# A feed-forward stage's VectorE order rearranged, with the low parts of 12 weight products moved from GpSimd to VectorE

## The reference, cut to what matters

```python
u = relu(rmsnorm(x, ln2) @ w_ff1)      # 1024 -> 4096
x = x + (u * u) @ w_ff2                # 4096 -> 1024
return rmsnorm(x, ln_f)
```

## Time and profile before

| | us |
|---|---|
| runs | 2685.26, 2678.33, 2684.0 |
| median | 2684.0 |
| the profiled execution, its own time | 2677.82 |
| its span, first to last instruction | 2676.0 |
| feed-forward stage in it, product 0 to the last matmul | 2019.6 to 2667.1 |

### The profile page before, as it was taken

How to read it: one execution, slowest core, us unless ns; L and a number is a source line. 1 busy time by engine, 2 the same in 40 slices (tenths; PEclk the granted TensorE clock), 3 DMA queues, 4 the chain that set the end, 5 groups by cost and what they waited for, 6 DMA issues and landing times. The chain is left out here.

```text
span 2676.0 us, 32703 instructions
## 1 busy us (share of the span) xinstructions
PE 2603.0 (97%) x13315; PEld 2193.7 (82%) x13315; DVE 1366.9 (51%) x1550; ACT 1094.1 (41%) x1700; POOL 814.7 (30%) x326
## 2 busy tenths in 40 slices
PE   7899999999999999999999999999998999999998
PEld 6688898898888888888888889888886788787877
DVE  3456633662332223564552667334427865838478
ACT  4356631111222212636563666333424535334344
POOL 1111112221222222422212225321423464555554
PEclk9899999999999999999999999999999999999999
DMA  3000011111111113222112113410125253351611
GB/s 134 24 25 25 25 40 48 47 48 40 44 51 41 50 48 112 73 105 71 40 40 87 53 49 131 165 56 32 40 79 216 99 202 144 126 220 34 249 63 63
DMA packets 68674, 216.77 MB, mean 81 GB/s; under 512 B 5476, under 2 KB 5860, under 8 KB 63672
## 3 DMA queue, kind: packets, MB, share of 16 engines
q1 hardware_dynamic: 63728, 190.53, 20.4%
q10 hardware_dynamic: 4808, 24.29, 2.4%
HBM read 185.23 MB, written 25.38 MB: 79 GB/s over the span
## 5 line engine op out<-in xcount | busy, mean ns | idle before, releaser
L711 POOL TENSOR_TENSOR w_lo<-w_raw,w_hi 128x1024 fp32r<-128x1024 f32 x144 | 349.0, 2424 | 1247.4 <-ACT w_hi L1862 1247.2
L851 POOL TENSOR_TENSOR ff_wl<-ff_raw,ff_wh 128x1024 fp32r<-128x1024 f32 x112 | 336.4, 3026 | 350.1 <-ACT ff_wh L2665 350.1
L864 PE MATMUL ps<-A_hi,w_hi 128*128 128x512 f32 (+2 forms) x1064 | 281.8, 357 | 0.0
L864 PE MATMUL ps<-A_lo,w_hi 128*128 128x512 f32 (+2 forms) x1064 | 279.3, 355 | 0.0
L864 PE MATMUL ps<-A_hi,w_lo 128*128 128x512 f32 (+2 forms) x1064 | 279.1, 354 | 0.0
L1862 ACT ACTIVATE w_hi<-w_raw 128x1024 fp32r<-128x1024 f32 x144 | 151.7, 1054 | 224.7 <-PE ps L864 131.2
L864 PEld LDWEIGHTS ps<-A_hi,w_hi 128*128 128x128 f32 x1064 | 182.7, 189 | 29.3 <-issue 1.9
L864 PEld LDWEIGHTS ps<-A_lo,w_hi 128*128 128x128 f32 x1064 | 182.8, 189 | 28.1
L864 PEld LDWEIGHTS ps<-A_hi,w_lo 128*128 128x128 f32 x1064 | 182.5, 189 | 27.9
L2665 ACT ACTIVATE ff_wh<-ff_raw 128x1024 fp32r<-128x1024 f32 x112 | 112.3, 1050 | 222.3 <-PE ps L1843 211.4
L1843 PE MATMUL ps<-ff_wh,A_hi 128*128 128x512 f32 x448 | 178.3, 398 | 13.6 <-DVE ff_y L3646 10.2
(11 more groups left out here) (530 smaller groups left out, 5920.5 us busy)
## 6 DMA issues: line engine op xcount, KB each, us to landing
w_raw<-in_units SPq DMA_DIRECT2D x144, 512.0 KB, 3.2
ff_raw<-in_blocks SPq DMA_DIRECT2D x32, 1024.0 KB, 4.8
A_hi<-token_operands SPq DMA_DIRECT2D x21, 1024.0 KB, 5.2
A_lo<-token_operands SPq DMA_DIRECT2D x21, 1024.0 KB, 7.2
token_operands<-A_hi SPq DMA_DIRECT2D x7, 1024.0 KB, 6.5
token_operands<-A_lo SPq DMA_DIRECT2D x7, 1024.0 KB, 8.2
X<-in_x ACTq DMA_DIRECT2D x4, 1024.0 KB, 12.1
X<-in_x ACTq DMA_DIRECT2D x1, 4096.0 KB, 15.4
```

Source lines behind the costliest of these rows:

```text
L711: nc.gpsimd.tensor_tensor(w_lo[:, slot, :], w_raw[:, slot, :], w_hi[:, slot, :].bitcast(F32), ALU.subtract).then_inc(w_lo_ready, 1)
L851: nc.gpsimd.tensor_tensor(ff_wl[n % 2][:, 2 * e:2 * e + 2, :], src[:, 2 * e:2 * e + 2, :], ff_wh[n % 2][:, 2 * e:2 * e + 2, :].bitcast(F32 ...
L864: last = nc.tensor.matmul(out, w[:, slot, o:o + m], v[:, k, cols] if k is not None else v[:, cols], start=(first and j == 0 and q == 0), s ...
```

## The change

- DVE makes the weights' low parts of the products n with m odd and j = 0, 1, 2 (12 of 56, in two halves each); `weight_low(n + 1)` stands right behind block 0's addition of product n. POOL skips them and waits, at the product after them, until they are all made.
- In iteration j = 0 of a second matrix the additions of blocks 0 and 1 move up among the sums: s3, block 0, low part, s2, block 1, s4, square_low(g, 2), block 2, block 3.
- Ahead of the stage ff_sum "c" and "e" move between ln2_low(5) and ln2_low(6), and token_low(0) moves between the two steps of `tok_t4`. ACT's token_high(0) moves from the end of iteration 0 into iteration 1, behind ff_high(2) and the last take of product 0. The norm's buffers swap places, so that ff_sum "e" overwrites only the gains and the squares.

```diff
+def ff_low_on_dve(n):
+
+    return n // 7 % 2 == 1 and n % 7 < 3
+
-        ln2_t = norm_temps("ln2", 49152)
+        ln2_t = (ar("ln2_g", 53248, [P, D]), ar("ln2_xn", 57344, [P, 2, D]), ar("ln2_sq", 49152, [P, D]))
...
                 src = ff_raw[FF_RAW[m][FF_ROLE[j]]]
+                if ff_low_on_dve(n):
+                    continue
+                if n and ff_low_on_dve(n - 1):
+                    pool.wait_ge(ff["wl"], fb["wl"] + 2 * n)
...
+                if n == 1:
+                    token_high(0)
                 for b in range(3):
                     ff_take(n, b)
-                if n < 4:
+                if 1 <= n < 4:
                     token_high(n)
...
             ln2.xn()
-            for o in range(4, ST):
-                ln2_low(o)
...
+            def weight_low(n):
+
+                src = ff_raw[FF_RAW[n // 7][FF_ROLE[n % 7]]]
+                for e in range(2):
+                    dve.wait_ge(ff["wh"], fb["wh"] + 2 * n + e + 1)
+                    if e == 0:
+                        dve.wait_ge(ff["wl"], fb["wl"] + 2 * n)
+                    v.tensor_tensor(ff_wl[n % 2][:, 2 * e:2 * e + 2, :], src[:, 2 * e:2 * e + 2, :],
+                                    ff_wh[n % 2][:, 2 * e:2 * e + 2, :].bitcast(F32), ALU.subtract).then_inc(ff["wl"], 1)
...
+            ln2_low(4)
+            ln2_low(5)
             dve.wait_ge(sw["w_xo"], 2 * ST)
-            dve.wait_ge(ff["t2"], fb["t2"] + 4)
             ff_sum(0, "c")
             ff_sum(0, "e")
+            ln2_low(6)
+            ln2_low(7)
+            dve.wait_ge(ff["t2"], fb["t2"] + 4)
             hi_21, lo_21 = (quadrant(a, 1).bitcast(F32) for a in (A_hi, A_lo))
             v.tensor_tensor(tok_t4[:, :, :], hi_21, tok_t2[:, :, :], ALU.subtract).then_inc(ff["t4"], 1)
+            token_low(0)
...
                 if second and j == 0:
-                    for kind in ("s3", "s2", "s4"):
-                        square_sum(g, kind, 1)
+                    square_sum(g, "s3", 1)
...
                 if taken:
                     ff_add(n, 0)
+                if n + 1 < FF_N and ff_low_on_dve(n + 1):
+                    weight_low(n + 1)
                 if first and j == 4:
                     square_low(g, 0)
+                if second and j == 0:
+                    square_sum(g, "s2", 1)
...
                 if second and j == 0:
+                    square_sum(g, "s4", 1)
                     square_low(g, 2)
...
-                if n < 4:
+                if 1 <= n < 4:
                     token_low(n)
```

## The result

The changed kernel takes 2652.5 us (median of 4 runs, 2650.6 to 2653.8) against 2682.8 (4 runs of the kernel before): ratio 0.989, 95% interval 0.987 to 0.990. The forecast was 2652.6.

What follows compares the result with a forecast made beforehand. PE works 97% of the span, so gains come only from its waits for late DVE work and its slow clock. Groups 23.3 plus start 8.1 make 31.4 us: 2684.0 to 2652.6, likeliest 2645 to 2660, range up to 2668.

Steps and rivals of the forecast that it cites:

- Groups, 23.3 us: Products 21 to 23 and their like: PE has no wait left, gain 5.8 us in each of four groups.
- What decides is the third block, not the late start: Product 22: its third block, waiting for DVE's addition, accounts for 5.57 of the 5.8 us lost per group.
- the clock's price was hidden: Product 22: the slow clock (0.87) behind the late start adds nothing beyond the third block's wait.
- Bounds of a low half 1.14 and 3.27, I take 1.14: Length in us of a low half on DVE: undisturbed 1.14, held 3.27; 1.14 taken because POOL is silent there.
- Start, 8.1 us: Products 1 to 3: 9.0 us lost at products 1 and 2 go, less 0.9 of new wait at product 3.
- 0.9 us of new wait: Product 3: POOL's second low half ends near 2059.7, PE wants it at 2058.8; bounds 0 and 3 us.
- sharing with token_low(1): Product 3's low part: POOL's second half shares with this DVE operation and ends near 2059.7.
- 0.61 of waiting for ACT: Ahead of product 1's first blocks: this wait of 0.61 us stays after the change.
- Rival A: Groups: DVE gains by POOL's silence exactly what the low parts cost it; only the start gains, 2676 us, chance 0.07.
- B: Low halves on DVE take 2.4 us, a group gains 2.2, 2667 us; chance 0.11 together with a failing start.
- C: DVE's long operations are not POOL's doing and low halves take 3.27 us: slower, 2728 us, chance 0.04.
- D: Product 22 waits for something else just behind DVE, such as ACT's high parts: no effect, 2684 us, chance 0.02.

Runs made afterwards that it cites:

- groups_only_b: Changed kernel with the start put back: old order of the norm's last tiles, first sums, token_low(0), token_high(0) and buffers; 2658.3 us, ratio 0.991 to the kernel before.
- pool_kept_busy: Changed kernel, but POOL does four unread 128x512 subtractions from constants wherever it skips a product's low part; 2670.8 us, ratio 0.996 to the kernel before.
- reorder_no_lows_b: Changed kernel with the new start and order of additions, but all 56 low parts on POOL; 2669.6 us, ratio 0.995 to the kernel before.
- after_again: The changed kernel itself, unedited, in a second set of runs beside its variants; 2651.9 us, ratio 0.989 to the kernel before.
- low3: Changed kernel, but DVE also makes the low part of product 3; 2647.6 us, ratio 0.987 to the kernel before.
- two_lows: Changed kernel, but DVE makes only the low parts of positions 0 and 1 of a second matrix; 2653.0 us, ratio 0.989 to the kernel before.
- position1_only: Changed kernel, but DVE makes only the low part of position 1 of a second matrix, 4 of 56 products; 2654.0 us, ratio 0.9895 to the kernel before.

## Why the prediction was right, and where it was not

- **Groups, 23.3 us: right, in size and in mechanism.** By time, groups_only_b gives 24.3; by stretch, 110.36 to 87.04. The terms one by one: a low pair 2.28 from its start to the next operation's (measured 2.27), square_low(g, 2) to 2.35 (2.36), s4 to 1.22 (1.23), sum "a" to 2.28 (2.28), 1.4 us to spare at the third block (1.7). pool_kept_busy shows that POOL's activity is what held DVE: with it back, and the low parts still on DVE, 18 of the 24 us are lost again.
- **What decides is the third block, not the late start: shown.** In reorder_no_lows_b product 22 waits 0.69 us at its start, not 3.18, and the group still loses 3.5 us or more. That the clock's price was hidden holds for three of the four groups. In the third the slow stretch was longer, product 36 had no wait at its third block and took 13.75 us and not 13.23, so 0.5 us there were the clock's:

```profile
2440.76:2454.51 13.75, 13.75 (x49) 11.11 (x49) 12.22 (x10) 3.19 (x4) 5.68 (x2) 0.79 0.00 1
```

- **"Bounds of a low half 1.14 and 3.27, I take 1.14": right**, because POOL was silent from product 20's pair to product 24's (37.27 us idle).
- **Start, 8.1 us: the mis-sized term.** Products 1 and 2 came as forecast: token_low(0) ended 10.3 us after product 1's start (10.7 forecast), 0.6 us before product 2 was due. The "0.9 us of new wait" at product 3 is the term that was too small. The wait alone was 2.52 to 2.65 us, and the product lost 3.0 us with it where the clock stayed at 1.00 (after_again) and 4.4 where it did not. The failing step is "sharing with token_low(1)": POOL's two halves met token_low(1) and also token_low(2), near the case that the prediction had as its bound of 3 us, and it had not counted the clock behind such a wait. low3 removes the meeting, and wait and slow stretch go with it. The "0.61 of waiting for ACT" that was to stay went: it stood ahead of product 1's fourth block, behind an ACT that sum "e" had held up, and product 1 now takes 10.88. So an execution without a slow stretch gains 58.28 - 51.73 = 6.6 us (after_again), close to the 6.8 by medians (4.0 to 9.1 from their interval); the profile after gained only 3.6, since product 0 and product 3 both ran in part at the low clock.
- **Rival A (the port moves, nothing else): fell.** Moving the pairs bought the groups' 23 to 24 us. DVE takes 1.14 us for a half, while a half on POOL cost it up to 2.2 (s4 at 3.42 against 1.22), whatever DVE happened to do. The Trainium skill, Perfetto Trace Analysis, section Optimizing Scalar/DVE Operations, says that offloading between these two might not help; in this direction it did.
- **Rivals B, C, D: fell.** The low halves have a length of 1.18 on average, not 2.4 or 3.27, and product 22 waits for nothing else.
- **The profiled execution** was forecast at 2646.4 and was 2653.8: 4.5 us from the start, 2.5 from the two slow stretches that this execution had and the one of before had not, 0.4 behind the last matmul. The 4.5 are 3.5 more than forecast at product 3 and 1.6 at product 0, less the 0.6 of ACT's wait. That the median fits to 0.1 us is luck: the gain was 30.3 and not 31.4, and the kernel before came out at 2682.8 and not at the 2684.0 from which the forecast was taken, so two errors of about 1.1 cancelled.
- The edit did more than these runs needed: 4 of the 12 moved low parts carry the gain of the groups, with 0.55 us to spare in place of 1.7, and the new order of the additions carries none of it once all 12 are moved.

## What to carry to other kernels

Where DVE is late and some of its operations have two lengths, look at what POOL does during the long ones: the cost of POOL's work is its own time plus what it makes DVE wait. Count the operations that meet on the way to the block that PE needs next; moving the one pair that meets them can be worth all of the stall, and moving more may buy nothing but margin. When a stall goes, the next wait on the same path is late by a similar meeting: follow it one product further before taking the gain as whole.

## What the runs showed of the hardware that was not expected

Whether a DVE operation is held by POOL turned on less than 0.1 us by the records. With POOL's instruction starting 0.46 us after the first of two DVE halves the second half was held (4.54 for the pair); with 0.54 us it passed (2.36) and POOL waited. It was so in every group: 0.46 or 0.47 and held in the four of reorder_no_lows_b, 0.53 or 0.54 and passed in the eight of two_lows and position1_only. The second half starts 1.14 us after the first, so a POOL instruction whose record began 0.60 us earlier did not yet keep DVE out. The Trainium skill, SBUF — State Buffer, section Who interferes with whom, says: "Issue order, not op shape, decides who blocks." The records of POOL's starts do not show that order to the tenth of a us, and how the two are arbitrated was not settled here.

PE's granted clock fell behind waits of 2.2 and 2.5 us in some executions, and stayed at 1.00 behind waits of 2.2 and 2.6 us in others. Behind the wait for tile 6 product 0 took 17.65 us in the changed kernel's profile and 16.07 in after_again's, with the same wait (2.16 and 2.17). Product 3 took 15.29 us with a wait of 2.52 and 13.90 with one of 2.65. A short wait's price was thus its length and up to 0.4 us, plus about 1.5 us where the clock fell.
